# Products into the state-space states in two parts, with stacked operands that pass through memory

## What is computed

```python
bu_re = jnp.einsum('blgh,gph->blgp', u, bb_re)   # u: (1, 256, 64 groups, 16)
bu_im = jnp.einsum('blgh,gph->blgp', u, bb_im)
_, _, s_re, s_im = lax.associative_scan(combine, (a_re, a_im, bu_re, bu_im), axis=1)
y = einsum('blgp,ghp->blgh', s_re, c_re) - einsum('blgp,ghp->blgh', s_im, c_im)
y = y.reshape(bsz, seq, S5_WIDTH) + d * xin      # then gelu and a gated product
```

## Time and profile before

| | |
|---|---|
| median of three runs | 2961.64 us |
| lowest, highest | 2961.48, 3687.77 us |
| profiled execution, its own time | 2961.87 us |
| its span | 2960.1 us |
| PE busy in the span | 2947.3 us (100%) |
| DVE busy | 1978.9 us (67%) |
| ACT busy | 1732.3 us (59%) |
| POOL busy | 440.4 us (15%) |
| granted clock of PE over the span | 1.00 |
| moved by the DMA engines | 588.43 MB, mean 199 GB/s |

### The profile page before, as it was taken

One profiled execution on the slowest core, in us unless ns is written; L12 is line 12 of the kernel. 1 busy time (PEld: TensorE's weight loads), 2 busy tenths in 40 slices (PEclk: granted clock), 3 DMA queues, 4 the chain that ended last, 5 costly groups with the idle time before them and its releaser, 6 DMA issues.

```text
span 2960.1 us, 37410 instructions
## 1 busy us (share of the span) xinstructions
PE 2947.3 (100%) x13302; PEld 2429.1 (82%) x13302; DVE 1978.9 (67%) x2104; ACT 1732.3 (59%) x2455; POOL 440.4 (15%) x422
## 2 busy tenths in 40 slices
PE   9999999999999999999999999999999999999998
PEld 7888888888888888888887788888888888888887
DVE  6767654566667777676778886555556666666666
ACT  6776644547655555555675576554557554555555
POOL 1000110110035243320235450110000000000000
PEclk9999999999999999999999999999999999999999
DMA  8656666756666676666765555766665666666664
GB/s 257 182 162 194 198 203 195 199 179 205 191 192 221 191 223 198 217 220 191 261 192 198 194 187 163 217 209 210 203 205 185 200 192 193 193 194 192 192 192 162
DMA packets 298845, 588.43 MB, mean 199 GB/s; under 512 B 18465, under 2 KB 18481, under 8 KB 298353
## 3 DMA queue, kind: packets, MB, share of 16 engines
q1 hardware_dynamic: 292352, 563.61, 61.6%
q0 software_dynamic: 5952, 22.77, 2.4%
q10 hardware_dynamic: 432, 0.62, 0.1%
HBM read 574.35 MB, written 12.58 MB: 198 GB/s over the span
## 4 chain that ended last, share of the span: by engine, by line
PE 95%; ACT 2%; DVE 1%; issue 1%; DMA 0%; SPq 0%; DVEq 0%; ACTq 0%
PE banks L1735 95%; ACT whi L616 1%; ACT L616 0%; PE banks L1738 0%; DVE W L1532 0%; DVE W L1524 0%; DMA raw<-in_w_in 0%; DVE banks L1525 0%; DVE wlo L1121 0%; ACT W L616 0%; DVE banks L1527 0%; ACT G L616 0%; DVE W L1547 0%; DVE W L1220 0%; ACT banks L616 0%
## 5 line engine op out<-in xcount | busy, mean ns | idle before, releaser
L1121 DVE TENSOR_TENSOR wlo<-raw,whi 128x1024 fp32r<-128x1024 f32 x1047 | 1354.1, 1298 | 875.7 <-ACT whi L616 869.2
L616 ACT ACTIVATE whi<-raw 128x1024 fp32r<-128x1024 f32 (+1 forms) x1049 | 1106.7, 1059 | 1041.9 <-PE banks L1735 979.0
L1735 PE MATMUL banks<-whi,Y 128*128 128x512 f32 x4800 | 1484.5, 389 | 0.3 <-DVE W L1220 0.2
L1735 PEld LDWEIGHTS banks<-whi,Y 128*128 128x128 f32 x4800 | 900.9, 188 | 188.3 <-issue 0.9
L1735 PE MATMUL banks<-wlo,Y 128*128 128x512 f32 x2400 | 933.7, 389 | 0.0
L1735 PE MATMUL banks<-whi,XH 128*128 128x512 f32 x1792 | 705.4, 394 | 2.1 <-DVE wlo L1121 1.9
L1735 PE MATMUL banks<-whi,XL 128*128 128x512 f32 x1792 | 698.1, 390 | 0.0
L1735 PE MATMUL banks<-wlo,XH 128*128 128x512 f32 x1792 | 697.6, 389 | 0.0
L1735 PEld LDWEIGHTS banks<-wlo,Y 128*128 128x128 f32 x2400 | 450.5, 188 | 93.2
L1735 PEld LDWEIGHTS banks<-whi,XH 128*128 128x128 f32 x1792 | 336.5, 188 | 78.7 <-issue 8.9
L1735 PEld LDWEIGHTS banks<-whi,XL 128*128 128x128 f32 x1792 | 336.3, 188 | 71.4
(11 more groups left out here) (256 smaller groups left out, 1191.4 us busy)
## 6 DMA issues: line engine op xcount, KB each, us to landing
raw<-in_w_in SPq DMA_DIRECT2D x383, 512.0 KB, 4.0
raw<-in_w_mlp_up SPq DMA_DIRECT2D x128, 512.0 KB, 3.9
raw<-in_w_mlp_down SPq DMA_DIRECT2D x128, 512.0 KB, 4.1
raw<-in_w_mlp_in SPq DMA_DIRECT2D x128, 512.0 KB, 3.8
raw<-in_w_mlp_out SPq DMA_DIRECT2D x128, 512.0 KB, 3.7
raw<-in_w_branch SPq DMA_DIRECT2D x80, 512.0 KB, 4.4
raw<-in_w_out SPq DMA_DIRECT2D x64, 512.0 KB, 4.5
tables<-G POOLq DMA_DIRECT2D x8, 1024.0 KB, 8.3
```

The source lines that it names most:

```text
L616: return nc.scalar.activation(out_, in_, f, **kw)
L1121: tt(wlo[:, i % RING, :], raw[:, i % RING, :], whi[:, i % RING, :].bitcast(F32), ALU.subtract)\
L1735: return nc.tensor.matmul(out_, l, r, start=start, stop=stop, **kw)
```

## The change

The four float32 products of a group become four products in fp32r over 128 rows. The 128 rows are four parts of 32 channels: the left operand holds B high, high, low, low, the right one u high, low, high, low, so one product sums all four cross products. The parts of B (4 MB as written, 1 MB each) and of u (2 MB) are made in SBUF, written to memory by SP's queue, and the stacks (256 KB of B and two loads of 128 KB of u for each of 16 groups) are fetched by POOL's queue.

```diff
+        SU = [slot(Y, 2)[:, CH * i:CH * i + CH].rearrange("p (e t) -> p e t", e=2) for i in range(2)]
+        SB = [slot(Y, 3)[:, CH * i:CH * i + CH].rearrange("p (r e s) -> p r e s", r=2, e=2) for i in range(2)]
+        SAVED = [64, 192, 320]
 (SyncE)
+            def s5_parts():
+                yield 14
+                sp_.wait_ge(S("s5_lo"), 2)
+                for part in range(4):
+                    sp_.dma_start(A["s5_b"][:, part].rearrange("m (c x) n -> m c x n", x=4),
+                                  (BHI, BLO)[part // 2].bitcast(F32)).then_inc(S("s5_saved"), 16)
+                yield 28
+                save_inputs(0)
+                yield 42
+                save_inputs(1)
+            def save_inputs(h):
+                sp_.wait_ge(S("s5_lo"), 3 + h)
+                for part, m in enumerate((UHI[h], ULO[h])):
+                    for c in range(4):
+                        sp_.dma_start(A["s5_u"][4 * h:4 * h + 4, c // 2, part, :, c % 2, :].rearrange("i c t -> c i t"),
+                                      m[32 * c:32 * c + 32].bitcast(F32).rearrange("p (i t) -> p i t", t=T)).then_inc(S("s5_saved"), 16)
 (GpSimd, block2)
+                pool.wait_ge(S("s5_saved"), SAVED[1])
+                load_stack(0)
+                load_stack(1)
                 for j in range(S5_TILES):
...
                     pool.wait_ge(S("s5_state_ready"), j + 1)
+                    if j % 2 and j < 29:
+                        m = (j + 3) // 2
+                        if m == 8:
+                            pool.wait_ge(S("s5_saved"), SAVED[2])
+                        pool.wait_ge(S("bu_mm"), 2 * m - 2)
+                        load_stack(m)
+            def load_stack(m):
+                pool.dma_start(slot(Y, 3)[:, CH * (m % 2):CH * (m % 2) + CH].bitcast(F32),
+                              A["s5_b"][m].rearrange("k c n -> (k c) n")).then_inc(S(f"s5_stack_in{m % 2}"), 16)
+                for d in range(2):
+                    pool.dma_start(slot(Y, 2)[64 * d:64 * d + 64, CH * (m % 2):CH * (m % 2) + CH].bitcast(F32),
+                                  A["s5_u"][m // 2, m % 2].rearrange("k c e t -> (k c) (e t)"))\
+                        .then_inc(S(f"s5_stack_in{m % 2}"), 16)
 (ScalarE, s5a)
+                for r in range(2):
+                    yield 4 + r
+                    act.wait_ge(S("s5_b_in"), 16)
+                    a(BHI[:, SL * r:SL * r + SL], BRAW[:, SL * r:SL * r + SL]).then_inc(S("s5_hi"), 1)
+                yield 21
+                act.wait_ge(S("stage_turned2"), 1)
+                a(UHI[0], UIN[0]).then_inc(S("s5_hi"), 1)
+                yield 29
+                act.wait_ge(S("stage_turned2"), 2)
+                act.wait_ge(S("c_scaled"), 1)
+                a(UHI[1], UIN[1]).then_inc(S("s5_hi"), 1)
 (VectorE)
-            def s5_g_lo():
+            def s5_lo():
+                for r in range(2):
+                    yield 6 + r
+                    dve.wait_ge(S("s5_hi"), 1 + r)
+                    c = slice(SL * r, SL * r + SL)
+                    tt(BLO[:, c], BRAW[:, c], BHI[:, c].bitcast(F32), ALU.subtract).then_inc(S("s5_lo"), 1)
+                for h in range(2):
+                    yield (22, 31)[h]
+                    dve.wait_ge(S("s5_hi"), 3 + h)
+                    tt(ULO[h], UIN[h], UHI[h].bitcast(F32), ALU.subtract).then_inc(S("s5_lo"), 1)
 (TensorE)
             def s5_in():
                 for m in range(16):
-                    yield S5Q + S5D * m
...
-                    if m == 0:
-                        pe.wait_ge(S("s5_b_in"), 32)
-                        pe.wait_ge(S("stage_turned2"), 1)
-                    else:
-                        if m == 8:
-                            pe.wait_ge(S("stage_turned2"), 2)
+                    yield S5Q + S5D * m + (0 if m else 2)
+                    pe.wait_ge(S(f"s5_stack_in{m % 2}"), 48 * (m // 2 + 1))
+                    if m:
                         pe.wait_ge(S("s5_r_ready"), 2 * m)
                     for r in range(2):
                         for e in range(2):
-                            c = c0 + 32 * e
-                            ins = mm(PU[e][:, T * r:T * r + T], BT[r][c:c + 32, i, :], XI[c:c + 32, i, :],
-                                     tile_position=(c, 0))
+                            ins = mm(PU[e][:, T * r:T * r + T], SB[m % 2][:, r, e, :], SU[m % 2][:, e, :])
```

More of the change, by code:

```diff
@@ L248, in build @@
         GMG = slot(W, 11)
-        BT = [slot(Z, 2 + r).rearrange("p (i c) -> p i c", i=8) for r in range(2)]
+        BRAW, BHI, BLO = slot(Z, 2, 2), slot(WR, 6, 2), slot(WR, 8, 2)
+        UIN, UHI, ULO = ([slot(t, i) for i in at] for t, at in ((W, (2, 3)), (WR, (4, 13)), (WR, (5, 5))))
+        SU = [slot(Y, 2)[:, CH * i:CH * i + CH].rearrange("p (e t) -> p e t", e=2) for i in range(2)]
+        SB = [slot(Y, 3)[:, CH * i:CH * i + CH].rearrange("p (r e s) -> p r e s", r=2, e=2) for i in range(2)]
         CT = [slot(Z, 8 + r).rearrange("p (i c) -> p i c", i=8) for r in range(2)]
@@ L402, in _ @@
                 branch = Steps(tables() if b == 2 else iter(()))
+                stacks = Steps(s5_parts() if b == 2 else iter(()))
                 for ph in "ab":
@@ L414, in _ @@
                             branch.upto(ch.u0 + i - u0[b, "a"])
+                            stacks.upto(ch.u0 + i - u0[b, "a"])
                 up = rows("w_mlp_up" if b == 1 else "w_mlp_in_2")
@@ L486, in block2 @@
                 pool.wait_ge(used, mlp_base(1, NF - 1))
+                pool.dma_start(BRAW, A["b_t"]).then_inc(S("s5_b_in"), 16)
                 for r in range(2):
[L488 to L491, removed]
+                    pool.dma_start(CT[r], A["c_t"][r]).then_inc(S("small2_in"), 16)
+                pool.dma_start(GW, A["gm_w_t"]).then_inc(S("small2_in"), 16)
                 pool.wait_ge(evict["dve"], down0[1] + NF * NCH)
-                pool.dma_start(A["x1"].rearrange("(t p) n -> p t n", p=P), X).then_inc(S("x_saved"), 16)
-                pool.wait_ge(S("gm_w_in"), 16)
+                pool.dma_start(A["x1"].rearrange("(t p) n -> p t n", p=P), X).then_inc(S("scratch_saved"), 16)
+                pool.wait_ge(S("small2_in"), 48)
                 nc.gpsimd.affine_select(out=GW, in_=GW, compare_op=ALU.is_ge, fill=0.0, base=0,
@@ L562, in make_tables @@
                         pool.dma_start(A["tables"][TG * g:TG * g + TG, :, i, :].rearrange("j p t -> p j t"), m)\
[L563 to L564 removed]
+                            .then_inc(S("scratch_saved"), 16)
+                pool.wait_ge(S("scratch_saved"), 32 * S5_TILES // TG)
             def load_bias(n, k):
@@ L1562, in gmlp @@
                 chain(nc.vector.reciprocal(grs, grs))
-                dve.wait_ge(S("gm_gain_in"), 16)
+                dve.wait_ge(S("gain_in"), 16)
                 for t in range(NT):
@@ L1691, in _ @@
                 gens = [Steps(g) for g in (([down_adds(b - 1)] if b != blocks[0] else []) + [x_lo(b, "a"), norm(b, "a"), evictions(b)] + (
-                    [stage_turn(), attn1(), attn1_y(), lru(), pool(), sconv(), s5_params()] if b == 1 else [stage_turn2(), s5(), attn2(), s5_g_lo(), gmlp(), glu_out()]) + [merge_turn(b), merge_lo(b)])]
+                    [stage_turn(), attn1(), attn1_y(), lru(), pool(), sconv(), s5_params()] if b == 1 else [stage_turn2(), s5(), attn2(), s5_lo(), gmlp(), glu_out()]) + [merge_turn(b), merge_lo(b)])]
                 boundary = [Steps(x_turn(b)), Steps(x_lo(b, "m")), Steps(norm(b, "m"))]
@@ L2122, in laid_out @@
             ct[r, q, :, :, :, q, :] = c[:, :, q].transpose(3, 0, 1, 2)
-    m["b_t"], m["c_t"] = bt.reshape(2, P, 8, P), ct.reshape(2, P, 8, P)
+    m["b_t"] = bt.reshape(2, 2, 2, 32, 8, P).transpose(4, 1, 3, 0, 2, 5).reshape(P, 2 * SL)
+    m["c_t"] = ct.reshape(2, P, 8, P)
     return m
@@ L2141 @@
     aps["tables"] = nc.dram_tensor("tables", (32, 128, 2, T), _mybir.dt.float32, kind="Internal").ap()
+    aps["s5_b"] = nc.dram_tensor("s5_b", (16, 4, 32, CH), _mybir.dt.float32, kind="Internal").ap()
+    aps["s5_u"] = nc.dram_tensor("s5_u", (8, 2, 2, 32, 2, T), _mybir.dt.float32, kind="Internal").ap()
     aps["x1"] = nc.dram_tensor("x1", (T, D), _mybir.dt.float32, kind="Internal").ap()
```

24 lines of the change are left out of this document (11 added, 13 removed).

## The result

The changed kernel takes 2967.8 us (median of 20 runs), the kernel before 2961.7 in the same session: a ratio of 1.002, 95% interval 1.0014 to 1.0026. It is 6 us slower, where 2.7 us faster was forecast, and 0.8 us above the upper end of the range. The profiled execution took 2966.67 us, 4.8 more than that of before, with a span of 2964.6, 4.5 more; its mean granted clock is 0.999.

The account below looks back on a forecast made before the run. PE's queue was taken to bound the kernel, tied with DVE and ACT in the second block's attention. Saving -8.0, first group's stall +4.6, copies of B +0.7: -2.7 us, forecast 2959 us, range 2953 to 2967.

Parts of the forecast that it names:

- the copies of B: Ahead of unit 15's load on SP's queue: 4.19 MB at 364 GB/s, load just in time; cost 0 to 2, taken 0.7 us.
- nothing in the change leaves PE idle for long: Whole span: granted clock 1.00 (2.4 GHz), so the clock was left out of the forecast.
- rival 2: At unit 15, copies of B move at 250 GB/s and hold up weights; PE stops about 5 us, 2963 to 2967; chance 0.17.
- POOL's issues: Three transfers behind every second tile; lateness falls on results needed a whole group later; cost 0, at most 1 us.
- rival 4: Other stretches absorb the saving too: DVE's spare falls 1.2 to 0.5, stall 0.3 to 0.5 a group; 2960 to 2964; chance 0.15.
- 8.0 us of saving: Shorter S5 products: 6.7 us from groups 0 to 9 plus 1.3 from groups 14 and 15, of 10.7 on PE.
- the eight saves in front of the load of unit 43: Among SP's 20 added transfers, 0.37 us each, 7.4 in three places; hidden, as loads are issued about three units early.
- The first group's stall: Moved first group: PE waits 2.1 us at unit 30, 1.9 at unit 31; together 4.6 us with later shortage, once.
- the new group: S5 group of four one-pass products of 256 columns: 0.47 us for itself, bounds 0.47 to 0.85.
- the stacks: POOL's transfers of stacked operands for each group land in time by some 4 us.
- the attention takes part back: Second block's attention, where DVE and ACT set the pace: 2.6 us of groups 10 to 13 turn into PE waits.
- DVE's rest of the second inputs: At position 31, DVE also has this rest, 1.23 us; by tile 3 another 0.6 us is short.

Follow-up runs that it names:

- experiment 4: Changed kernel with the four copies of B issued one at a time at positions 14, 17, 20 and 23 instead of all at 14: 2963.12 us, ratio 1.0006.
- experiment 5: Changed kernel with POOL issuing each stack behind the even tile instead of the odd tile: 2965.51 us, ratio 1.0013.
- experiment 7: Changed kernel with copies of B issued one at a time and stacks issued behind POOL's even tile: 2961.32 us, ratio 0.9999.
- experiment 2: Kernel before plus POOL's three transfers, of numbers nobody reads, behind each odd tile up to tile 13: 2961.53 us, ratio 1.0.
- experiment 3: Kernel before with first S5 group two units later and POOL's three unread transfers behind odd tiles up to 13: 2965.76 us, ratio 1.0015.
- experiment 9: Changed kernel with the old float32 products on 32 rows in its S5 groups; waits, copies and transfers unchanged: 2972.73 us, ratio 1.0036.
- experiment 1: Kernel before with only its first S5 group moved two units later, behind unit 28: 2965.54 us, ratio 1.0014.
- the kernel with the three edits: Changed kernel with copies of B spread, stacks issued behind the even tile, DVE's tiles 0 and 1 behind unit 31: 2958.89 us, ratio 0.9991.
- the last version: The kernel with the three edits, plus second saves spread, first inputs' rest at 21, saves at 26, group 0 behind unit 27, DVE's first tiles at 30: 2955.68 us.

## Why the prediction was wrong

The step that failed is the one on the copies of B: "Just in time: cost 0 to 2, I take 0.7". By medians they cost 4.7 (experiment 4). I had taken the load as served when the copies alone would be done, at about 1473; the queue also held 1.7 MB of other loads, and it landed at 1477.05, though the rate was as high as I assumed (356 GB/s against 364). The clock's fall behind the wait, which I had excluded with "nothing in the change leaves PE idle for long", adds 1.6 us where it comes. The price is that of rival 2, about 5 us, but not its condition, a rate of 250 GB/s; of what stood for that rival it was the one queue. It is then chance that the total lies close to its 2963 to 2967, since the other misses below are in it as well.

The second failed step: POOL's issues, "Cost 0, at most 1". They cost 2.3 by the medians of experiment 5, 1.8 by those of 4 and 7, and 2.7 in the table between units 32 and 92. Their delay falls not on a result that is needed late but on DVE's rest by way of the lock, and only where DVE is late (experiments 2, 3, 5, 7): with the shorter products at four groups up to 1700 us, with the old ones and the change's other additions at two (experiment 9). So rival 4, DVE without spare, came true in part beside the rest: the changed kernel keeps 4.7 of the 8.0 us of saving. A third: the eight saves in front of the load of unit 43, "this is hidden". Once POOL's issues are out of the way they cost 1.6; in the changed kernel they hide behind the other waits.

Right were: the new group (1517.63 to 1518.11, so 0.48 us to the next unit, forecast 0.47); the first group's stall, forecast 4.0 at units 30 and 31 and found at 3.96 in experiment 1 (3.4 of it in the two waits themselves); the stacks, for which PE never waits; and that the attention takes part back: forecast 2.6, found 1.3 to 1.8 (the column of units 92 to 152 against 187.44 less 1.3; the kernel with the three edits has 3.0 there, 1.2 of it by the fall of its clock). The 8.0 us of realised saving were nearly to be had: the last version is 6.65 ahead in the table and 5.8 by medians, with 0.6 still lost at its first groups (45.31 against 45.97 less 1.3). The changed kernel kept 4.7.

The sum again, in us against before. With the old products the changed kernel has, in the table, the late group's +4.0 (49.98 against 45.97), +1.5 between units 32 and 92 and +0.5 behind; the copies are +4.7 by medians; the products give back the 4.7 of experiment 9. That makes 6.0, and 6.1 was measured. Against the forecast the copies cost 4.0 more, the products give 3.3 less, and the late group with what follows it costs 6.0 in place of 4.6: 8.7 of the 8.8 us between -2.7 and 6.1. The +1.5 stand at units 36 and 41 (waits of 0.67 and 0.25 us, behind rests of 2.86 and 2.83). Experiment 3 found none of it for the late group and the issues alone, so it takes something more. DVE's rest of the second inputs, of which I had reckoned 0.6 us by tile 3, is the likely thing; no run takes it out, and that stays open.

## What to carry to other kernels

Big saves on a queue that also carries the just-in-time loads hold up the load behind them (here 12.2 us from issue to landing in place of 4.0), together with whatever else the queue already holds; issue them in pieces between the loads, and count all the bytes in front of a load, not the new ones alone. An engine's spare at one place (POOL's gap, DVE's 1.2 us) is spare only while its partner is on time: when a change shortens the bounding engine's work, recheck which partner is now late, and what of its work the side engines then run into. Test each part alone and in the changed kernel: here POOL's issues cost nothing in the old kernel and 2.3 us in the new one. And look at the granted clock before a difference of 1 or 2 us in a single profile is read as a cause: in two rows of the table a fall that costs 1.6 us looks like rival B, and the medians don't have it.

## What was unexpected of the hardware

Of four transfers of 1 MB in a row, the first two kept SP for 0.6 us each and the third and fourth for 2.2 (1.8 and 1.9 in experiment 9), against 0.37 for a load of 512 KB, and the loads right behind took up to 1.5 us to issue (1.9 in experiment 9). Behind a wait of PE the granted clock fell to 0.50 for 3.4 us in five of fourteen profiles, after waits of 3.62, 2.31, 2.00 (twice) and 1.84 us and after two of 0.58 and 0.81 close together, and it did not after others of 2.82, 2.21 and 2.00 (twice). A DVE subtraction from SBUF took 1.23, 1.78 or 2.87 us depending on which POOL instruction it met.
